# Gated DeltaNet branch: one set of scores for both directions, and the second triangular inverse on GpSimd

## The chip, the cores and the metric

One core of one Trainium2 chip runs the whole layer. The time is device time in microseconds (us), the median of three runs. 128 partitions; TensorE, VectorE (DVE), ScalarE (ACT), GpSimd (POOL) and SyncE (SP) each work through their own instructions in order and wait for each other by semaphores.

## The reference, cut to what matters

The reference is one layer of a bidirectional encoder: four branches over 1,024 tokens, a gated merge, cross-attention to a memory, a mixture of 32 experts. The change lies in branch D, the gated DeltaNet with four heads of 64, which runs over the sequence forward and backward and adds the two:

```python
kk = jnp.einsum('bhntd,bhnsd->bhnts', kc, kc)
a_mat = jnp.where(strict, bc[..., None] * kk * decay, 0.0) + jnp.eye(c)
sol = lax.linalg.triangular_solve(a_mat, rhs, left_side=True, lower=True, unit_diagonal=True)
qk = jnp.einsum('bhntd,bhnsd->bhnts', qc, kc) * decay
...
v_new = u_i - jnp.einsum('bhtd,bhde->bhte', kc_i, state)
o = jnp.einsum('bhtd,bhde->bhte', qd_i, state) + jnp.einsum('bhts,bhse->bhte', qk_i, v_new)
state = cd_i[..., None, None] * state + jnp.einsum('bhsd,bhse->bhde', kd_i, v_new)
```

For each chunk, the scores k k' and q k' are scaled by the decay exp(gam_t - gam_s) below the diagonal (above it, for the backward direction), a unit triangular matrix is inverted, and a recurrence carries the state from chunk to chunk. The scores of a chunk are the same for both directions; decay, mask and beta differ.

## The kernel before, in words

One list of steps, written by hand in `plan_schedule`, sets the order of every engine: each engine walks it and does its own part of each step. `dense(...)` interleaves the steps of a stage with the dense matmuls of other panels: each `None` in the list lets out one part, six matmuls of 128x512 for a `gate` (four parts a group) or `up` group (one part), with the ScalarE and VectorE work that belongs to it: weight conversion (L1349, L1965), the tanh of a gate (L1375), the eviction and addition of an `up` group (L1988, L1994). The two PSUM banks of the dense groups alternate, so TensorE waits when an eviction two groups back is late.

The DeltaNet works in eight chunks of 128 tokens, T/128 = `TT`. Three stages matter.

`gdn_a` prepares. In iteration i the forward direction has chunk i and the backward direction chunk 7 - i; each has PSUM banks of its own. GpSimd subtracts gamma from its broadcast row and masks the result (L2813, L2816, step part 0), ScalarE takes exp of it into `NQT` (L1716), TensorE makes the scores (L991, part 1), VectorE multiplies exp by beta (L2387) and both by the scores (L2395, marks `lt` and `qt`). `NLT` and `NQT` of one iteration lie in the buffer `LQ`, two of them in turn. ScalarE copies the 32x32 diagonal blocks out (L1728, part 2) and writes `LQ` to DRAM (`gdn_out`, L1763). Since exp writes into `NQT`, ScalarE waits in front of exp for the write of two iterations before (`lq_out`).

The inverse. The diagonal blocks of four iterations are a half b (0 or 1): `gdn_ship` writes them to DRAM (L1767), `gdn_read` reads them back with one block in each partition (L1777), `gdn_inv` inverts all 128 at once on VectorE, row by row:

```python
for j in range(first_row, next_row):
    n = 31 - j
    V.tensor_tensor(part, bc(U[:, j + 1:32, j:j + 1], P, n, j), bc(U[:, j:j + 1, 0:j], P, n, j), ALU.mult)
    V.tensor_tensor(U[:, j + 1:32, 0:j], U[:, j + 1:32, 0:j], part, ALU.subtract)
```

(L2407 and L2410, n times j elements a partition, 30 rows; each waits for the one before). Each half is cut into ten steps of three rows, in front a copy (L2402), at the end L2413, L2415 and two memsets. `gdn_back` writes the result to DRAM (L1783). Half 0 is inverted during `gdn_a` and after it, half 1 during the first three iterations of `gdn_c`.

`gdn_c` is the recurrence, eight iterations of seven parts. `gdn_load` and `gdn_load_inv` read `LQ` and the inverses from DRAM (L1793, and four issues of L1803 an iteration, all on ScalarE's queue). GpSimd spreads the 32x32 inverses into block diagonal matrices (L2825, part 0, two for each direction) and scales the keys (L2843, L2845, part 1); TensorE merges the blocks up to 128x128 (L1015, L1024, L1031, with a ScalarE copy L1751 in front of L1038) and does the products with the state (L1038 to L1066). Around the steps of `gdn_c` stands one None each, and in iterations 0 to 2 five more.

## Time and profile before

| what | us |
|---|---|
| median of three runs | 2041.04 (2040.80 to 2041.76) |
| the profiled execution, its own time | 2028.88 |
| its span | 2027.1 |
| TensorE busy | 1878.2 |
| VectorE, ScalarE, GpSimd busy | 1384.4, 1078.0, 308.8 |
| the stage `gdn_a`, first score matmul to last dense one before the next gap | 675.9 to 739.1 |
| the stage `gdn_c`, first matmul to last | 778.9 to 951.0 |

The profile records one execution. Busy time is what an engine spends in instructions; TensorE's ends are modelled. The mean granted clock of TensorE is 0.977 of full speed. Times in the rows below are counted from the start of the span. A wait is put down to what ended last before the engine went on.

### The profile page before, as it was taken

The page shows a single profiled execution, that of the slowest core. Times are in us where ns is not written, and L with a number is a line of the kernel's source. Part 1 is how long each engine was busy: PE and PEld are TensorE (multiplying, and loading weights), DVE is VectorE, ACT ScalarE, POOL GpSimd, SP SyncE. Part 2 cuts the span into 40 slices and gives each one's busy share as a digit, 9 for nine tenths or more (in the row PEclk, how much of TensorE's full clock was granted, in tenths as well). Part 3 has the DMA queues.
Part 4 walks back from the last instruction along what each step waited for, and adds up shares of the span by engine and source line. Part 5 has one row for each costly group of instructions (what it writes and reads, how often), then busy time and mean ns, then how long its engine had stood idle before and what let it go on. Part 6 is the DMA issues. An engine that isn't in the chain of part 4 may idle for free.

```text
span 2027.1 us, 32760 instructions
## 1 busy us (share of the span) xinstructions
PE 1878.2 (93%) x12949; PEld 1117.6 (55%) x12949; DVE 1384.4 (68%) x1833; ACT 1078.0 (53%) x1568; POOL 308.8 (15%) x269
## 2 busy tenths in 40 slices
PE   6999999999999989899999999995899999999991
PEld 3464565655544545677488755684455444444440
DVE  5555533799974797544733745437799999999997
ACT  4573223566646541223433533334588888888873
POOL 5000100344310512231000000000000111111103
PEclk9999999999999999999999999997899999999996
DMA  5411111212011562441522510404799999999986
GB/s 193 159 52 43 32 42 48 73 48 58 22 28 47 194 201 79 142 122 45 213 65 67 157 32 16 169 32 161 279 422 422 422 422 422 422 422 423 422 346 269
DMA packets 145817, 366.80 MB, mean 181 GB/s; under 512 B 39296, under 2 KB 94880, under 8 KB 119072
## 3 DMA queue, kind: packets, MB, share of 16 engines
q1 hardware_dynamic: 96608, 279.57, 36.3%
q10 hardware_dynamic: 40240, 52.50, 7.7%
q0 software_dynamic: 8848, 33.03, 4.2%
q8 instruction: 86, 1.41, 0.3%
q14 instruction: 35, 0.29, 0.0%
HBM read 314.14 MB, written 46.73 MB: 178 GB/s over the span
## 4 chain that ended last, share of the span: by engine, by line
PE 77%; DVE 10%; ACT 5%; issue 4%; DMA 2%; ACTq 1%; SPq 1%; DVEq 0%; POOLq 0%
PE psum L794 39%; PE psum L1185 24%; ACT arena L1631 2%; PE psum L1174 1%; PE psum L1109 1%; PE psum L1084 1%; DVE arena L2308 1%; PE psum L924 1%; PE psum L1203 1%; PE psum L811 1%; DMA gdn_lq<-arena 1%; PE psum L1066 1%; PE psum L1044 1%; DMA arena<-in_w_in_dram 1%; PE psum L935 1%
## 5 line engine op out<-in xcount | busy, mean ns | idle before, releaser
L794 PE MATMUL psum<-arena 128*128 128x512 f16 (+2 forms) x6000 | 1013.4, 326 | 17.6 <-ACT arena L1375 6.8
L794 PEld LDWEIGHTS psum<-arena 128*128 128x128 f16 x6000 | 567.6, 98 | 398.6 <-issue 15.6
L1185 PE MATMUL psum<-arena 128*128 128x512 f16 x2304 | 512.3, 381 | 14.7 <-issue 11.7
L751 DVE SCALAR_TENSOR_TENSOR arena<-arena 128x2048 f16<-128x2048 f32 x192 | 437.3, 2286 | 58.0 <-ACT arena L745 57.8
L745 ACT ACTIVATE arena<-arena 128x2048 f16<-128x2048 f32 x192 | 365.3, 1908 | 72.4 <-DMA arena<-in_w_dram 43.2
L1185 PEld LDWEIGHTS psum<-arena 128*128 128x128 f16 x2304 | 224.5, 98 | 280.4 <-issue 22.1
L1965 DVE SCALAR_TENSOR_TENSOR arena<-arena 128x512 f16<-128x512 f32 (+1 forms) x185 | 125.8, 699 | 114.0 <-ACT arena L1349 113.5
L2862 POOL DMA_INDIRECT arena<-xhat,arena x32 | 66.2, 2069 | 839.8 <-PE psum L1174 445.2
L1349 ACT ACTIVATE arena<-arena 128x512 f16<-128x512 f32 (+1 forms) x212 | 127.2, 616 | 51.5 <-issue 19.9
L1375 ACT ACTIVATE arena<-psum,arena 128x512 f32<-128x512 f32 x60 | 41.0, 684 | 140.3 <-PE psum L794 139.6
L1438 ACT ACTIVATE arena<-psum 128x512 f32<-128x512 f32 (+3 forms) x51 | 29.9, 586 | 126.4 <-PE psum L794 126.4
L1403 ACT ACTIVATE arena<-arena 128x256 f32<-128x256 f32 x64 | 26.7, 416 | 109.7 <-DVE arena L2000 108.6
L2757 POOL TENSOR_SCALAR arena<-arena 128x512 f32<-128x512 f32 x27 | 57.5, 2130 | 138.3 <-ACT arena L1349 138.3
L2293 DVE CUSTOM_DVE_ANT_0 arena<-psum,arena 128x1024 f32<-128x1024 f32 x64 | 75.6, 1219 | 2.3 <-PE psum L911 2.2
L1631 ACT ACTIVATE arena<-arena 128x1024 f32<-128x1024 f32 x64 | 72.9, 1147 | 7.3 <-DVE arena L2293 7.2
L1988 DVE SCALAR_TENSOR_TENSOR arena<-arena,psum 128x512 f32<-128x512 f32 x64 | 43.8, 684 | 42.7 <-PE psum L794 31.9
L2000 DVE SCALAR_TENSOR_TENSOR arena<-psum,arena 128x512 f32<-128x512 f32 x32 | 22.1, 690 | 65.1 <-PE psum L794 65.1
L2018 DVE SCALAR_TENSOR_TENSOR arena<-psum,arena 128x512 f16<-128x512 f32 x36 | 24.8, 690 | 59.9 <-ACT arena L1438 31.0
L1640 ACT ACTIVATE arena<-psum 128x512 f16<-128x512 f32 x64 | 34.7, 594 | 55.1 <-PE psum L924 34.3
L2825 POOL TENSOR_TENSOR arena<-arena 128x512 f32<-128x512 f32 x32 | 34.5, 1109 | 144.5 <-PE psum L1052 92.4
L1880 ACT ACTIVATE arena<-psum 128x512 f32<-128x512 f32 x64 | 38.2, 597 | 13.9 <-PE psum L1185 13.1
L1174 PE MATMUL psum<-arena 128*128 128x128 f32 x256 | 34.5, 279 | 8.8 <-DMA arena<-xhat,arena 8.8
(388 smaller groups left out, 2017.4 us busy)
## 6 DMA issues: line engine op xcount, KB each, us to landing
arena<-in_w_dram SPq DMA_DIRECT2D x192, 1024.0 KB, 11.9
arena<-in_merge_w_dram SPq DMA_DIRECT2D x64, 256.0 KB, 3.2
yrows<-arena ACTq DMA_DIRECT2D x32, 512.0 KB, 7.8
arena<-in_w_in_dram SPq DMA_DIRECT2D x48, 256.0 KB, 2.8
gdn_lq<-arena ACTq DMA_DIRECT2D x8, 1024.0 KB, 4.5
arena<-gdn_lq ACTq DMA_DIRECT2D x8, 1024.0 KB, 5.0
arena<-in_xattn_wkv_dram SPq DMA_DIRECT2D x32, 256.0 KB, 3.0
yrows<-arena POOLq DMA_DIRECT2D x1, 7680.0 KB, 24.1
```

The costliest lines, as they stand in the source:

```text
L745: nc.scalar.activation(half_of(pieces(e, m)[0], half), half_of(XLAND[m], half), ACT.Copy, scale=WS).then_inc(w_hi[m], 1)
L751: nc.vector.scalar_tensor_tensor(half_of(lo, half), half_of(XLAND[m], half), WS, half_of(hi, half), ALU.mult, ALU.subtract).then_inc(w_lo[ ...
L794: mm = nc.tensor.matmul(bank[prt[0]:prt[1], c0:c1], lhs[a](k), rhs[b](k), start=(k == 0 and a + b == 0), stop=(k == nk - 1 and a == 1))
L1174: tr = nc.tensor.transpose(PS[:, k // 4, (k % 4) * P:(k % 4) * P + P], xs[:, k, :], ident)
L1185: mm = nc.tensor.matmul(PS[:, bank, :], left[a][:, k, :], right[b][:, k, columns], start=k + a + b == 0, stop=(k == n - 1 and a == 1))
L1349: S.activation(W[i % 2][0][:, 2 * j:2 * j + 2, 0:wide], LAND[c % NLAND][:, :, 0:wide], ACT.Copy, scale=WS).then_inc(*act_hi.mark(c))
L1631: S.activation(DS[u % 2][:, m, :], DS[u % 2][:, m, :], ACT.Exp, scale=-1.0, bias=d_mx[u % 2][:, m:m + 1], accum_out=d_l[u % 2][:, m:m + 1])\
L1965: V.scalar_tensor_tensor(W[i % 2][1][:, 2 * j:2 * j + 2, 0:wide], LAND[c % NLAND][:, :, 0:wide], WS, W[i % 2][0][:, 2 * j:2 * j + 2, 0:wid ...
L1988: V.scalar_tensor_tensor(dst, gate, 1.0, bank, ALU.add, ALU.mult).then_inc(*e.mark(n))
L2293: V.tensor_tensor_reduce(out=DS[u % 2][:, m, :], in0=PS[:, 2 + 2 * m:4 + 2 * m, :].rearrange("p a b -> p (a b)"), in1=DWH[:, 896 - P * qt: ...
L2757: G.tensor_scalar(landed_c, landed_c, WS, None, ALU.mult).then_inc(*counter("pool_w_scaled").mark(chunk))
L2862: G.indirect_dma_start(XR[e % 2], None, XH_D, bass.IndirectOffsetOnAxis(IDX[:, e:e + 1], 0)).then_inc(rows_in[e % 2], 16)
```

## The change

- `gdn_a` takes one chunk an iteration for both directions, in the order `CH` = 0, 7, 1, 6, 2, 5, 3, 4. One set of scores is made for it; the banks now alternate by iteration. `AT` says in which iteration a chunk was prepared, and the writes of `LQ` and of the inverses and the rows of `GDIAG` are put so that `gdn_c` finds both directions of its iteration together. `gdn_out` issues two writes of half the size.
- exp goes into the buffer `NY`. ScalarE no longer waits there for `lq_out`, but for `qt` of the iteration before; VectorE waits for `lq_out` in front of its first product.
- `gdn_inv` of half 1 is one step of all thirty rows and runs on GpSimd. It stands behind `gdn_read` 1 and in front of `gdn_c` 0. `gdn_read` 1 moves up between the pieces of half 0; `gdn_back` 1 moves to iteration 0, part 3, and has four writes of 64 partitions, as has `gdn_back` 0.
- `gdn_load_inv` has two reads for each iteration instead of four.
- The Nones are dealt anew: more between the pieces of half 0, none extra in `gdn_c`.

The diff, with its indentation taken off and lines of context cut; the other hunks put the new marks and counts of the semaphores into waits:

```diff
@@ -260,19 +260,16 @@
...
 for i in range(TT):
-    mid = {6: inv(0, 2)}.get(i, [])
-    gdn += [("gdn_a", i, 1)] + {6: inv(0, 1), 7: inv(0, 4)}.get(i, []) + [None] + [("gdn_a", i + 1, 0), None] * (i + 1 < TT) + mid
-    gdn += [("gdn_a", i, 2), ("gdn_out", i)] + [("gdn_ship", 0)] * (i == 3) + [None]
-    gdn += {4: [("gdn_read", 0), None], 5: inv(0, 0) + [None], 6: inv(0, 3) + [None], 7: [("gdn_ship", 1)]}.get(i, [])
-for p in range(5, 10):
-    gdn += inv(0, p) + [None] * (2 + (p < 8)) + [("gdn_load", p - 5)] * (p < 7)
-gdn += [("gdn_back", 0)] + [None] * 6 + [("gdn_load_inv", 0), ("gdn_load_inv", 1), ("gdn_read", 1)] + [None] * 7
+    gdn += [("gdn_a", i, 1)] + {6: inv(0, 0), 7: inv(0, 2)}.get(i, []) + [None] + [("gdn_a", i + 1, 0), None] * (i + 1 < TT)
+    gdn += [("gdn_a", i, 2), ("gdn_out", i)] + {3: [("gdn_ship", 0)], 6: inv(0, 1), 7: [("gdn_ship", 1), None]}.get(i, []) + [None]
+    gdn += [("gdn_read", 0), None] * (i == 4) + [None] * (i >= 6)
+for p in range(3, 10):
+    gdn += inv(0, p) + [None] * (2 + (p > 3)) + [("gdn_load", p - 7)] * (p in (7, 8)) + [("gdn_read", 1), ("gdn_inv", 1, 1, 31)] * (p == 4)
+gdn += [("gdn_back", 0)] + [None] * 5 + [("gdn_load_inv", 0), ("gdn_load_inv", 1)] + [None] * 5
 for i in range(TT):
     for part in range(7):
-        gdn += [("gdn_back", 1)] * ((i, part) == (3, 1))
-        gdn += [("gdn_c", i, part)] + [None] * (1 + (i < 3 and part in (1, 4) and (i, part) != (2, 1)))
-        if i < 3 and part in (1, 2, 4) or (i, part) == (0, 5):
-            gdn += inv(1, 3 * i + (i > 0) + (1, 2, 4, 5).index(part))
+        gdn += [("gdn_back", 1)] * ((i, part) == (0, 3))
+        gdn += [("gdn_c", i, part), None]
         if part == 2 and i and i + 1 < TT:
@@ -467,6 +464,8 @@
...
 NGR = [[f32(BR + 8192 + 1024 * j + 512 * d, NH, P) for d in range(2)] if j < 2 else (NX, NZ_)[j % 2] for j in range(TT)]
+CH = [c for k in range(TT // 2) for c in (k, TT - 1 - k)]
+AT = [CH.index(i) for i in range(TT)]
 GDIAG = [f32(UN + 5120 + 1024 * b, 32, 32) for b in range(2)]
@@ -975,23 +974,21 @@
...
     q, v, a, po = (counter(f"{e}_gdn") for e in ("pe", "vec", "act", "pool"))
-    for d in range(2):
-        c = i if d == 0 else TT - 1 - i
-        cs = slice(c * P, c * P + P)
-        B0, B1, B2 = (PS[:, 2 + 3 * d + b, :].rearrange("p (h n) -> p h n", h=NH) for b in range(3))
-        if part == 1:
-            if i == 0 and d == 0:
-                pe.wait_ge(*counter("act_gdnp").at("tm", "nv", 3))
-                pe.wait_ge(*counter("act_gdnp").at("egrows"))
-            if i:
-                pe.wait_ge(*v.at("qt", i - 1, d))
-            for t in range(4):
-                for u, bank in enumerate((B1, B2)):
-                    hp = slice(64 * u, 64 * u + 64)
-                    mm = nc.tensor.matmul(bank[:, t, :], NK[hp, t % 2, cs], (NK if t < 2 else NQ)[hp, t % 2, cs],
-                                          start=True, stop=True)
-                    if t == 3:
-                        mm.then_inc(*q.mark("qk", i, d, u))
+    cs = slice(CH[i] * P, CH[i] * P + P)
+    B1, B2 = (PS[:, 3 + 3 * s + b, :].rearrange("p (h n) -> p h n", h=NH) for b in range(2))
+    if part == 1:
+        if i == 0:
+            pe.wait_ge(*counter("act_gdnp").at("tm", "nv", 3))
+            pe.wait_ge(*counter("act_gdnp").at("egrows"))
+        if i >= 2:
+            pe.wait_ge(*v.at("qt", i - 2, 1))
+        for t in range(4):
+            for u, bank in enumerate((B1, B2)):
+                hp = slice(64 * u, 64 * u + 64)
+                mm = nc.tensor.matmul(bank[:, t, :], NK[hp, t % 2, cs], (NK if t < 2 else NQ)[hp, t % 2, cs],
+                                      start=True, stop=True)
+                if t == 3:
+                    mm.then_inc(*q.mark("qk", i, u))
 elif what == "gdn_c":
@@ -1434,7 +1431,7 @@
...
             elif name == "nz":
-                act.wait_ge(inv_out[1], 32)
+                act.wait_ge(inv_out[1], 64)
         S.activation(dst, src, ACT.Copy, scale=1 / WS).then_inc(*e.mark(n))
@@ -1703,29 +1700,32 @@
...
         for d in range(2):
-            r0 = 32 * d + 4 * (j if d == 0 else TT - 1 - j)
+            r0 = 32 * d + 4 * CH[j]
             S.dma_start(NGR[j][d], A["gdn_rows"][0, r0:r0 + 4].partition_broadcast(P)).then_inc(gam_in[j], 16)
...
         for d in range(2):
-            c = i if d == 0 else TT - 1 - i
             act.wait_ge(*po.at("low", i, d))
-            after(act, lq_out[i % 2], 16 * (i // 2))
-            S.activation(NQT[i % 2][d], NGR[i][d], ACT.Exp).then_inc(*a.mark("dt", i, d))
+            if i:
+                act.wait_ge(*v.at("qt", i - 1, d))
+            else:
+                act.wait_ge(*counter("act_gdnp").at("tm", "nv", 3))
+            S.activation(NY[d], NGR[i][d], ACT.Exp).then_inc(*a.mark("dt", i, d))
         j = i + 2
...
                 act.wait_ge(*(a.at("dt", j - 2, d) if j >= 4 else counter("act_gdnp").at("tm", "nv", 3)))
-                r0 = 32 * d + 4 * (j if d == 0 else TT - 1 - j)
+                r0 = 32 * d + 4 * CH[j]
                 S.dma_start(NGR[j][d], A["gdn_rows"][0, r0:r0 + 4].partition_broadcast(P)).then_inc(gam_in[j % 2], 16)
...
                 bp = slice(32 * b, 32 * b + 32)
-                S.activation(GDIAG[i // 4][bp, 16 * d + 4 * (i % 4):16 * d + 4 * (i % 4) + 4, :], NLT[i % 2][d][bp, :, bp], ACT.Copy)\
+                u0 = 16 * d + 4 * ((i ^ d) % 4)
+                S.activation(GDIAG[i // 4][bp, u0:u0 + 4, :], NLT[i % 2][d][bp, :, bp], ACT.Copy)\
                     .then_inc(*a.mark("diag", i, d, b))
@@ -1760,7 +1760,8 @@
...
     act.wait_ge(*counter("vec_gdn").at("qt", i, 1))
-    S.dma_start(A["gdn_lq"][i], LQ[i % 2]).then_inc(lq_out[i % 2], 16)
+    for d in range(2):
+        S.dma_start(A["gdn_lq"][i ^ d, :, 1024 * d:1024 * d + 1024], LQ[i % 2][:, 1024 * d:1024 * d + 1024]).then_inc(lq_out[i % 2], 16)
 elif what == "gdn_ship":
@@ -1778,30 +1779,31 @@
...
     b = step[1]
-    act.wait_ge(*counter("vec_gdn").at("inv", b))
+    act.wait_ge(*counter("pool_gdn" if b else "vec_gdn").at("inv", b))
     for n, m in enumerate((NU[b], NUT[b])):
-        S.dma_start(A["gdn_inv"][b, n].rearrange("u (b f) -> (u b) f", b=4), m.rearrange("p r c -> p (r c)")).then_inc(inv_out[b], 16)
+        for d in range(2):
+            S.dma_start(A["gdn_inv"][b, n].rearrange("(k e h) (b f) -> e k (h b) f", e=2, h=NH, b=4)[d],
+                        m[64 * d:64 * d + 64].rearrange("p r c -> p (r c)")).then_inc(inv_out[b], 16)
 elif what == "gdn_load":
...
     q = counter("pe_gdn")
-    act.wait_ge(lq_out[s], 16 * TT // 2)
+    act.wait_ge(lq_out[s], 32 * TT // 2)
     if i < 2:
...
         act.wait_ge(*q.at("o", i - 2, 1))
-    S.dma_start(LQ[s], A["gdn_lq"][i]).then_inc(lq_in[s], 16)
+    S.dma_start(LQ[s], A["gdn_lq"][AT[i]]).then_inc(lq_in[s], 16)
 elif what == "gdn_load_inv":
...
     s = i % 2
-    act.wait_ge(inv_out[i // 4], 32)
+    b, k = divmod(AT[i], 4)
+    act.wait_ge(inv_out[b], 64)
     if i >= 2:
...
     for n in range(2):
-        for d in range(2):
-            u0 = 16 * d + 4 * (i % 4)
-            S.dma_start(XZC[s][:, 8 * n + 4 * d:8 * n + 4 * d + 4, :],
-                        A["gdn_inv"][i // 4, n, u0:u0 + 4].rearrange("u (p c) -> p u c", c=32)).then_inc(lq_in[s], 16)
+        S.dma_start(XZC[s][:, 8 * n:8 * n + 8, :],
+                    A["gdn_inv"][b, n, 8 * k:8 * k + 8].rearrange("u (p c) -> p u c", c=32)).then_inc(lq_in[s], 16)
 elif what == "merged_pair":
@@ -2378,22 +2380,21 @@
...
     for d in range(2):
-        c = i if d == 0 else TT - 1 - i
-        B1, B2 = (PS[:, 3 + 3 * d + b, :].rearrange("p (h n) -> p h n", h=NH) for b in range(2))
         if part == 1:
...
                 dve.wait_ge(*a.at("diag", i - 2, d, 3))
-            V.tensor_tensor(NLT[s][d], NQT[s][d], bc(BES[:, d, c, :].unsqueeze(2), P, NH, P), ALU.mult)\
+                dve.wait_ge(lq_out[s], 32 * (i // 2))
+            V.tensor_tensor(NLT[s][d], NY[d], bc(BES[:, d, CH[i], :].unsqueeze(2), P, NH, P), ALU.mult)\
                 .then_inc(*v.mark("dt1", i, d))
             dve.wait_ge(*v.last())
-            BB = PS[:, 3 + 3 * d:5 + 3 * d, :]
+            BB = PS[:, 3 + 3 * s:5 + 3 * s, :]
             for u in range(2):
-                dve.wait_ge(*q.at("qk", i, d, u))
-            for n, (of, to) in enumerate((("lt", NLT), ("qt", NQT))):
-                both = to[s][d].rearrange("p (u t) n -> p u (t n)", u=2)
-                V.tensor_tensor(both, BB[:, :, 256 * n:256 * n + 256], both, ALU.mult).then_inc(*v.mark(of, i, d))
-elif what == "gdn_inv":
+                dve.wait_ge(*q.at("qk", i, u))
+            for n, (of, to, by) in enumerate((("lt", NLT[s][d], NLT[s][d]), ("qt", NQT[s][d], NY[d]))):
+                to, by = (m.rearrange("p (u t) n -> p u (t n)", u=2) for m in (to, by))
+                V.tensor_tensor(to, BB[:, :, 256 * n:256 * n + 256], by, ALU.mult).then_inc(*v.mark(of, i, d))
+elif what == "gdn_inv" and not step[1]:
     b, first_row, next_row = step[1:]
@@ -2815,6 +2816,30 @@
...
                             pattern=[[0, NH], [-1 if d else 1, P]], channel_multiplier=1 if d else -1).then_inc(*po.mark("low", i, d))
+elif what == "gdn_inv" and step[1]:
+    b, first_row, next_row = step[1:]
+    po = counter("pool_gdn")
+    U, UT = NU[b], NUT[b]
+    if first_row == 1:
+        pool.wait_ge(diag_in[b], 32)
+        pool.wait_ge(*counter("act_gdn").at("dt", TT - 1, 1))
+        G.tensor_copy(U[0:64], UT[0:64].rearrange("p r c -> p c r")).then_inc(*po.mark("forward", b))
+        pool.wait_ge(*po.last())
+    for j in range(first_row, next_row):
+        n = 31 - j
+        part = NX[0].rearrange("p h n -> p (h n)")[:, 0:n * j].rearrange("p (r c) -> p r c", c=j)
+        G.tensor_tensor(part, bc(U[:, j + 1:32, j:j + 1], P, n, j), bc(U[:, j:j + 1, 0:j], P, n, j), ALU.mult)\
+            .then_inc(*po.mark("term", b, j))
+        pool.wait_ge(*po.last())
+        G.tensor_tensor(U[:, j + 1:32, 0:j], U[:, j + 1:32, 0:j], part, ALU.subtract).then_inc(*po.mark("row", b, j))
+        pool.wait_ge(*po.last())
+    if next_row == 31:
+        G.tensor_scalar(UT, U.rearrange("p r c -> p c r"), -1.0, None, ALU.mult).then_inc(*po.mark("turned", b))
+        pool.wait_ge(*po.last())
+        G.tensor_scalar(U, U, -1.0, None, ALU.mult).then_inc(*po.mark("negative", b))
+        pool.wait_ge(*po.last())
+        for m in (U, UT):
+            G.memset(m.rearrange("p r c -> p (r c)")[:, ::33], 1.0).then_inc(*po.mark(*(("inv", b) if m is UT else ("one", b))))
 elif what == "gdn_c":
```

## Rows read from the trace of the kernel before

**Rows 1.** The page: TensorE's busy share, and the chain by engine.

```profile
PE 1878.2 (93%) x12949; PEld 1117.6 (55%) x12949; DVE 1384.4 (68%) x1833; ACT 1078.0 (53%) x1568; POOL 308.8 (15%) x269
...
PE 77%; DVE 10%; ACT 5%; issue 4%; DMA 2%; ACTq 1%; SPq 1%; DVEq 0%; POOLq 0%
```

**Rows 2.** Windows: us, busy us (instructions) per engine, granted clock, DMA share, GB/s.

```profile
675.90:739.10 63.20, 57.00 (x431) 32.94 (x430) 52.68 (x84) 31.37 (x80) 24.32 (x25) 0.97 0.61 200
739.10:745.30 6.20, 0.06 (x2) 0.03 (x2) 5.92 (x13) 4.18 (x11) 0.00 (x0) 0.94 0.40 148
...
778.90:802.90 24.00, 24.00 (x275) 15.93 (x275) 19.76 (x51) 4.93 (x11) 6.47 (x8) 1.00 0.14 46
...
912.10:932.20 20.10, 20.10 (x273) 17.81 (x273) 8.59 (x25) 5.26 (x12) 6.42 (x9) 1.00 0.35 107
932.20:951.00 18.80, 18.80 (x259) 16.84 (x259) 7.36 (x21) 3.38 (x8) 1.13 (x2) 1.00 0.03 9
```

**Rows 3.** TensorE's waits from 675 to 955: us in total, times, longest.

```profile
PE psum L794 <- DVE arena L1988: 6.1, 1, 6.1
PE psum L1038 <- ACT arena L1751: 5.2, 3, 2.2
PE psum L794 <- ACT arena L1375: 4.9, 2, 2.6
PE psum L991 <- DVE arena L2395: 3.6, 4, 1.3
```

**Rows 4.** Timeline of TensorE: start, us, instructions, [idle before <- releaser].

```profile
722.78 2.06 PE L991 MATMUL psum<-arena 64*128 64x128 f32 x32
...
745.28 28.67 PE L794 MATMUL psum<-arena 128*128 128x512 f16 x126 [6.14 <-DVE arena L1988]
```

**Rows 5.** All waits from 675 to 955, ScalarE's for the write.

```profile
ACT arena L1716 <- DMA gdn_lq<-arena: 15.0, 6, 3.7
```

**Rows 6.** Timeline of VectorE in gdn_a.

```profile
677.86 1.11 DVE L2387 TENSOR_TENSOR arena<-arena 128x512 f32<-128x512 f32 x1
...
682.44 0.95 DVE L2387 TENSOR_TENSOR arena<-arena 128x512 f32<-128x512 f32 x1
...
687.44 0.69 DVE L1994 TENSOR_TENSOR arena<-arena 128x512 f32<-128x512 f32 x1
...
716.99 1.34 DVE L1994 TENSOR_TENSOR arena<-arena 128x512 f32<-128x512 f32 x1
...
740.70 1.29 DVE L2395 TENSOR_TENSOR arena<-psum,arena 128x512 f32<-128x512 f32 x2
```

**Rows 7.** DMA issues from 660 to 960: count, KB each, median us to landing.

```profile
gdn_lq<-arena ACTq DMA_DIRECT2D x8, 1024.0 KB, 4.5
...
gdn_diag<-arena ACTq DMA_DIRECT2D x2, 512.0 KB, 6.6
arena<-gdn_diag ACTq DMA_DIRECT2D x4, 256.0 KB, 5.0
```

**Rows 8.** Timeline of GpSimd in two stretches.

```profile
16.20 1.48 POOL L2757 TENSOR_SCALAR arena<-arena 128x512 f32<-128x512 f32 x1
17.77 1.91 POOL L2759 TENSOR_TENSOR arena<-arena 128x512 f16<-128x512 f32 x1
...
716.75 1.04 POOL L2813 TENSOR_TENSOR arena<-arena 128x512 f32<-128x512 f32 x1 [5.35 <-DMA arena<-gdn_rows]
...
847.89 0.61 POOL L2843 TENSOR_TENSOR arena<-arena 128x256 f32<-128x256 f32 x1 [0.67 <-DVE arena L2451]
...
864.80 4.03 POOL L2825 TENSOR_TENSOR arena<-arena 128x512 f32<-128x512 f32 x4 [13.96 <-PE psum L1052]
```

**Rows 9.** Groups on VectorE from 720 to 765: busy, mean ns, idle before.

```profile
L2410 DVE TENSOR_TENSOR arena<-arena 128x30 f32<-128x30 f32 (+14 forms) x30 | 10.0, 332 | 1.0
L2407 DVE TENSOR_TENSOR arena<-arena 128x30 f32<-128x30 f32 (+14 forms) x30 | 9.9, 330 | 0.8
```

**Rows 10.** Window just behind the gap that ends at 745.3.

```profile
745.00:746.00 1.00, 0.72 (x2) 0.28 (x3) 0.96 (x3) 0.00 (x0) 0.00 (x0) 0.50 0.95 275
```

8 lines of the change are left out of this document (4 added, 4 removed).

## The prediction

> **What bounds the kernel now.** I read the page's busy shares and its chain first: TensorE is busy 93% of the span and carries 77% of the chain [rows 1]. So a change pays only where it removes work from TensorE or closes a gap in it. Then the table of windows over the DeltaNet stage [rows 2]. Its preparation (`gdn_a`, 675.9 to 739.1) has 57.00 us of TensorE in 63.20, and the next window is a pure gap of 6.2. The recurrence (`gdn_c`, 778.9 to 951.0, eight windows) costs 24.0 us in its first iteration, 20.1 when undisturbed and 18.8 in the last. The list of TensorE's waits [rows 3] says which waits end last: 6.1 us on VectorE's eviction of an `up` group, queued behind pieces of the first inverse; 4.9 and 3.6 on ScalarE and VectorE while `gdn_a` runs; 5.2 on the ScalarE copy L1751, behind which stand the issues of reads. Together about 21 us of idle time. ScalarE itself waits six times for the write of `gdn_lq` [rows 5].
>
> **Fill.** Each None of the order lets out six matmuls (128x512), 1.28 us when they stream: 126 of them took 28.67 us [rows 4], of which about 1.5 us was the low level of the clock. I counted the Nones from `gdn_a` 0 to the last `gdn_c`: 117 in both orders. So the fill is moved, not added, and the time changes by TensorE's saved work plus the difference in its gaps.
>
> **1. One set of scores.** An iteration issues 16 instead of 32 score matmuls. 32 took 2.06 us [rows 4], so half is 0.95 to 1.03 and eight iterations save about 8 us of TensorE.
>
> **2. Exp into NY, no wait for the DMA in front of it.** Before, ScalarE issued the write of `gdn_lq`, waited for its landing and only then did exp, the diagonal copies and the next write: `gdn_a` ran at about 8.5 us an iteration (`qt` 0 ends at 682.4, `qt` 7 at 742.0, [rows 6]). After it, exp waits for VectorE's `qt` of the iteration before, and VectorE waits for the write of two iterations before. VectorE's own work is then 4.6 us (from one L2387 to that of the next iteration, [rows 6], iteration 0) plus 1.2 for evictions and low parts of three Nones, 5.8 in all. The DMA loop needs 0.65 exp, some 1.0 until the write is issued, 4.5 to land [rows 7] and 4.6 of VectorE over two iterations, so it hardly binds; at worst (6.5 an iteration) it costs 5 us more. The doubled write issues are ScalarE sequencer time beside its own diagonal copies: nothing, at most a microsecond in all. From 682.4, six iterations on is 717.2; then two pieces of inverse 0 (copy 1.1 and twelve short operations, 4.9) and the last iteration: `qt` 7 at 727.5 instead of 742.0. TensorE gains some of this at once, but what counts is what is late next.
>
> **3. The second inverse on GpSimd.** It stands in GpSimd's queue in front of the spreads L2825 of `gdn_c` 0, and TensorE waits for those. So its length decides. Its start: diagonal copies about 1 us after `qt` 7, the ship to DRAM 6.6, the read back issued and landed, 5.0 plus 1 for its second half [rows 7]: 727.5 + 14 to 15 = about 742.
> Its length: for j = 1 to 30 two operations of j(31-j) elements each, 60 instructions and 9,920 elements. The trace has no such short GpSimd operation. The nearest rows are tensor_tensors of 256 elements at 0.61 us and of 512 at 1.04 [rows 8], so 1.68 ns an element and 0.18 fixed; a dependent one starts 0.08 later (16.20 + 1.48 to 17.77). 60 x 0.26 + 16.7 = 32.3 us. The pattern broken in runs of 32 (L2825, four in 4.03) is no slower; runs of one to 30 are not shown. The two closing tensor_scalars of 1,024 elements follow L2757, 1.48 for 512: 2.8 each. Copy and memsets 1.8. Sum 40 us alone. From below I take 36 (closing ones and gaps cheap), from above 62 (short runs at a little over half the rate).
> Contention: L1994 on VectorE took 1.34 us instead of 0.69 (as at 687.44) because it stood until GpSimd's L2813 had ended [rows 6, 8]; so the two exclude each other for operations with two SBUF inputs. During GpSimd's first 24 us VectorE still does 30 operations of inverse 0 (60 of them are 19.9 us, [rows 9]). If they take turns, each GpSimd operation loses about 0.2: 6 us. Later evictions cost 2 more. I take 48.5, and add 2 for the first two spreads: `gdn_c` 0 starts on TensorE at 742 + 48.5 + 2 = 793.
> The Trainium skill (SBUF — State Buffer, the part on the shared port pair) says the pair is an exclusive lock held for a whole instruction; the trace agrees in L1994's 1.34 us, and it speaks against moving an inverse beside the other.
>
> **4. What covers it.** From `gdn_read` 1 to `gdn_c` 0 lie 25 Nones, 32 us. TensorE reaches the read at about 735 and `gdn_c` 0 at 768. Inverse 0, slowed by the turns, ends at about 763; its write and reads, at 4 to 5 us each like those of [rows 7], and their issue allow the start at 775 at the latest, so it stays in front of GpSimd. TensorE stands 20 to 25 us. After such a gap the granted clock is low (0.50 behind the gap of 6.1 us, [rows 10]) and gives away 1.5 us more.
>
> **5. The recurrence.** VectorE loses 20 us of inverse work there, but was not its bound: the fill removed (five Nones, 6.4 us) is time that TensorE spent earlier. Of the 6.2 us of gaps, fewer reads (two instead of four issues an iteration) and a free VectorE take 4; the four issues of `gdn_back` 1, now in front of L1751 in iteration 0, give 1.5 back. 172.1 - 6.4 - 2.5 = 163.2.
>
> **Sum.** 793 + 163.2 + 1.5 = 957.7 where the recurrence ended at 951.0: +6.7 us. Behind it everything shifts along. On the profiled span 2027.1 becomes 2033.8 (its time 2028.88 becomes 2035.6). The profiled execution lies 12 us under the median of the runs; I put the difference on the median: 2041 + 7 = 2048.
>
> **Rivals.**
> A, my forecast: GpSimd's inverse is later than its cover. 2048, own range 2042 to 2056. Chance 0.48.
> B, the other side: the inverse on GpSimd is done in 30 us or less, or nearly so. Then inverse 0's way through DRAM sets the start at about 773 and the end is 773 + 163.2 = 936 to 938: -13, 2028. It decides below 42 us of length, where the sum is nil. For it speaks that the row of 0.61 us may hold more pipeline time than I think, and that some closing operations are single-input; against, that 16.7 us for the elements alone is measured rate. Chance 0.28 for the side below 42, some of it near no change.
> C, short runs cost extra on GpSimd: 62 us, `gdn_c` 0 at 806, +20, 2061. Nothing in the trace shows runs under 32. Chance 0.16.
> The Trainium skill (GPSIMD Engine Reference, section 3.1) states 2.6 cycles an element at 1.2 GHz for two inputs, 2.17 ns; the trace shows 1.68 ns. As an estimate by that page the elements take 21.5 us instead of 16.7 and the end is 2053, between A and C.
> D, `gdn_a` is not quicker, because ScalarE, now held by VectorE's `qt`, or the write still sets 8 us an iteration: everything in A starts 10 us later, 2058. For it speaks that out, exp and `dt1` still form a loop over two iterations; against, the sum of 13 us or less for two. Chance 0.08.
>
> **Numbers.** 0.2% is 4 us, about what a measurement of this kernel can tell from no change. A lies above it in about 0.38 and within it in 0.10; B faster in 0.23, within in 0.05; C and D slower. Faster 0.24, same 0.16, slower 0.60. The range takes both ends of the length, from B's 2029 to C's 2062.
>
> **What would show it.** Right: L991 with 128 instructions; no wait of L1716 for `gdn_lq`; `qt` 7 near 728; the GpSimd chain from about 742 for 45 to 55 us without a gap; one TensorE wait of 20 us or more on GpSimd in front of the first L1015; recurrence of 162 to 164 us. Wrong: GpSimd operations of 240 elements far from 0.58 us, no such wait, or `gdn_a` still at 8 us an iteration.

## The result, and the profile after

The changed kernel takes 2072.72 us (median of 4 runs, 2071.38 to 2075.02) against 2040.92 for the kernel before (4 runs, 2037.04 to 2041.76). The ratio is 1.0153, with a 95% interval of 1.0127 to 1.0178: 26 to 36 us slower. The prediction was 2048, with a range of 2029 to 2062: the sign was right, the size was not, and the time lies above the range. The profiled execution has a span of 2070.4 us (its time 2072.16).

Where the time lies is read off the stage's ends. In the windows below gdn_c ends at 977.0, where it was 951.0: +26.0 of the stage. What comes behind can't be compared between these two profiled executions: from there to the end of the span it is 1076.1 us before and 1093.4 after, but among the experiments below, which change next to nothing there, it lies between 1078 and 1093 (1089.6 in before_two_exp, the kernel nearest to before). So 26 us are located and the rest of the median's 31.8 (some 5 us, no more than the interval leaves open) is not.

The windows of the stage (us; busy us and instructions of TensorE, its weight loads, VectorE, ScalarE, GpSimd; granted clock as a share of full speed; DMA share; GB/s): gdn_a, the way to gdn_c 0, gdn_c 0, gdn_c 1, and the other six.

```profile
678.00:744.20 66.20, 48.29 (x264) 22.33 (x263) 45.94 (x76) 32.84 (x85) 23.67 (x24) 0.85 0.64 191
744.20:807.90 63.70, 46.47 (x189) 19.05 (x188) 43.29 (x75) 10.54 (x19) 45.21 (x68) 0.89 0.47 128
807.90:836.10 28.20, 23.48 (x227) 15.24 (x227) 8.55 (x23) 3.73 (x9) 10.26 (x13) 0.88 0.14 48
836.10:857.00 20.90, 20.45 (x229) 14.13 (x229) 9.05 (x24) 5.57 (x12) 6.43 (x9) 1.00 0.41 114
857.00:977.00 120.00, 119.09 (x1442) 91.33 (x1442) 48.72 (x136) 28.06 (x61) 34.50 (x42) 1.00 0.35 104
```

Against [rows 2] TensorE has less to do in gdn_a, as meant, but the stretch is no shorter and its clock is 0.85 instead of 0.97. It then takes 63.7 us from the last `qt` to gdn_c 0, where it took 37 (742.0 to 778.9). gdn_c 0 costs 28.2 instead of 24.0.

TensorE's waits from 675 to 1010 (us in total, times, longest), and three waits of the others from 675 to 808:

```profile
PE psum L793 <- ACT arena L1372: 26.4, 6, 6.2
PE psum L793 <- DVE arena L1990: 8.1, 2, 5.4
PE psum L1035 <- ACT arena L1751: 4.0, 2, 3.1
PE psum L1012 <- POOL arena L2850: 2.0, 2, 1.6
```

```profile
DVE arena L1967 <- ACT arena L1346: 38.5, 8, 10.9
...
ACT arena L1715 <- DVE arena L2396: 26.2, 11, 4.6
...
ACT arena L1372 <- issue: 15.8, 2, 14.4
```

[Rows 3] held four small waits; now one line dominates, ScalarE's gate tanh L1372: 17.9 of its 26.4 us lie in gdn_a (four times), 8.5 on the way to gdn_c 0 (twice). GpSimd, which was to be the late one, has 2.0 us. ScalarE waits for VectorE's `qt` in front of exp (L1715), VectorE waits for ScalarE's high part L1346 (18.6 of the 38.5 us up to the last `qt`), and nobody waits for the write of `gdn_lq` any more, as ScalarE did in [rows 5]. "issue" means that the profile shows no wait; the 14.4 us in front of L1372 are explained further down.

One iteration of gdn_a, all engines (start, us, what; idle before and releaser in brackets):

```profile
695.50 1.29 DVE L2396 TENSOR_TENSOR arena<-psum,arena 128x512 f32<-128x512 f32 x2
...
696.88 0.63 ACT L1715 ACTIVATE arena<-arena 128x512 f32<-128x512 f32 x1 [2.10 <-DVE arena L2396]
696.90 0.96 ACTq L1721 DMA_DIRECT2D arena<-gdn_rows  x2
...
697.91 1.30 ACT L1728 ACTIVATE arena<-arena 32x128 f32<-32x128 f32 x4 [0.40 <-ACT arena L1715]
...
699.57 0.97 ACT L1728 ACTIVATE arena<-arena 32x128 f32<-32x128 f32 x3
700.57 0.63 ACT L1346 ACTIVATE arena<-arena 128x512 f16<-128x512 f32 x1
701.10 0.67 ACT L1372 ACTIVATE arena<-psum,arena 128x512 f32<-128x512 f32 x1
701.23 0.69 DVE L1967 SCALAR_TENSOR_TENSOR arena<-arena 128x512 f16<-128x512 f32 x1 [4.44 <-ACT arena L1346]
...
701.83 1.03 PE L793 MATMUL psum<-arena 128*128 128x512 f16 x2 [6.10 <-ACT arena L1372]
701.84 0.68 DVE L2388 TENSOR_TENSOR arena<-arena 128x512 f32<-128x512 f32 x1
```

This is a ring. (A None's weight conversion has a high part on ScalarE, L1346, and a low part on VectorE, L1967, which waits for it. Line numbers shift by a few from kernel to kernel.) The last `qt` (to 696.8) lets exp go; behind exp in ScalarE's order stand the issues, the eight diagonal copies and the high part; VectorE, whose low part L1967 stands ahead of its next `dt1`, has nothing to do for 4.44 us; TensorE, whose next group needs the gate tanh, nothing for 6.10. Then VectorE works and ScalarE waits. `dt1` starts at 682.2, 692.1, 701.8 and 711.6: 9.8 us an iteration. That is the ring's own pace. Not every iteration has it: the second `qt` comes only 4.0 us behind the first, and the fifth iteration takes 12.3 us, with slower issues of `gdn_rows` (1.90 us) and the two of `gdn_read` (2.2) in ScalarE's order. From the first iteration's `qt` to the last, seven iterations take 8.8 us each on average, where they took 8.5 before.

The second inverse on GpSimd (first instructions, the middle, the end), and ScalarE's queue around the two writes of inverses:

```profile
757.75 1.94 POOL L2826 COPY arena<-arena 64x1024 f32<-64x1024 f32 x1 [31.09 <-DMA arena<-gdn_diag]
759.78 0.29 POOL L2831 TENSOR_TENSOR arena<-arena 128x30 f32<-128x30 f32 x1
...
777.54 0.61 POOL L2831 TENSOR_TENSOR arena<-arena 128x240 f32<-128x240 f32 x1
778.23 0.65 POOL L2834 TENSOR_TENSOR arena<-arena 128x240 f32<-128x240 f32 x1
...
780.48 1.29 POOL L2831 TENSOR_TENSOR arena<-arena 128x238 f32<-128x238 f32 x1
...
798.79 3.63 POOL L2837 TENSOR_SCALAR arena<-arena 128x1024 f32<-128x1024 f32 x1
802.50 3.04 POOL L2839 TENSOR_SCALAR arena<-arena 128x1024 f32<-128x1024 f32 x1
```

```profile
782.59 5.08 ACTq L1785 DMA_DIRECT2D gdn_inv<-arena  x4
799.12 2.39 ACTq L1805 DMA_DIRECT2D arena<-gdn_inv  x4
...
817.86 4.91 ACTq L1785 DMA_DIRECT2D gdn_inv<-arena  x4
```

GpSimd needs 757.75 to 805.8, 48.0 us, with the durations that the prediction gave it. But the second fence holds what it did not see: four writes, each of 64 partitions of one of the two matrices, keep ScalarE's issue for 5.08 us, and from the first of them to the first read that waits for them are 16.5 us. The kernel before issued two writes (0.82 us at 763.93) and the reads 4.7 us later. ScalarE stands in this stretch twice: before 782.6 it waits some 9 us for VectorE's first inverse, which with the 5.08 us of issues makes the 14.4 us "issue" in front of L1372; and from 789.0 to 799.1 it waits for the writes to land, and can do no high part meanwhile.

### The profile page after: what moved, and what is told of

Same layout as the page of the kernel before. It is cut to its first block, busy times and chain, and to the rows that moved or that the text cites. A ratio compares the mean times of both kernels' runs of the same rounds, so it can differ in the third digit from the quotient of the medians.

```text
span 2070.4 us, 32498 instructions
## 1 busy us (share of the span) xinstructions
PE 1884.4 (91%) x12821; PEld 1112.7 (54%) x12821; DVE 1365.5 (66%) x1768; ACT 1079.2 (52%) x1568; POOL 348.8 (17%) x334
## 4 chain that ended last, share of the span: by engine, by line
PE 76%; DVE 8%; ACT 5%; issue 5%; POOL 2%; DMA 2%; ACTq 1%; DVEq 1%; SPq 1%; POOLq 0%
PE psum L793 38%; PE psum L1182 24%; ACT arena L1628 2%; PE psum L1171 1%; PE psum L1106 1%; PE psum L1081 1%; DVE arena L2310 1%; POOL arena L2831 1%; PE psum L923 1%; POOL arena L2834 1%; ACT arena L1728 1%; PE psum L1200 1%; PE psum L810 1%; PE psum L1063 1%; PE psum L1041 1%
## 5 line engine op out<-in xcount | busy, mean ns | idle before, releaser
L793 PE MATMUL psum<-arena 128*128 128x512 f16 (+2 forms) x6000 | 1029.0, 329 | 41.2 <-ACT arena L1372 28.3
L750 DVE SCALAR_TENSOR_TENSOR arena<-arena 128x2048 f16<-128x2048 f32 x192 | 437.3, 2286 | 57.6 <-ACT arena L744 57.5
L1967 DVE SCALAR_TENSOR_TENSOR arena<-arena 128x512 f16<-128x512 f32 (+1 forms) x185 | 123.2, 686 | 138.0 <-ACT arena L1346 137.6
L2887 POOL DMA_INDIRECT arena<-xhat,arena x32 | 65.5, 2048 | 842.2 <-PE psum L1171 445.9
L1346 ACT ACTIVATE arena<-arena 128x512 f16<-128x512 f32 (+1 forms) x212 | 127.0, 616 | 60.6 <-issue 24.7
L1372 ACT ACTIVATE arena<-psum,arena 128x512 f32<-128x512 f32 x60 | 41.0, 684 | 152.6 <-PE psum L793 136.7
L1990 DVE SCALAR_TENSOR_TENSOR arena<-arena,psum 128x512 f32<-128x512 f32 x64 | 43.8, 684 | 40.2 <-PE psum L793 26.9
```

Of the source, the lines that this page charges most:

```text
L750: nc.vector.scalar_tensor_tensor(half_of(lo, half), half_of(XLAND[m], half), WS, half_of(hi, half), ALU.mult, ALU.subtract).then_inc(w_lo[ ...
L793: mm = nc.tensor.matmul(bank[prt[0]:prt[1], c0:c1], lhs[a](k), rhs[b](k), start=(k == 0 and a + b == 0), stop=(k == nk - 1 and a == 1))
L1346: S.activation(W[i % 2][0][:, 2 * j:2 * j + 2, 0:wide], LAND[c % NLAND][:, :, 0:wide], ACT.Copy, scale=WS).then_inc(*act_hi.mark(c))
L1967: V.scalar_tensor_tensor(W[i % 2][1][:, 2 * j:2 * j + 2, 0:wide], LAND[c % NLAND][:, :, 0:wide], WS, W[i % 2][0][:, 2 * j:2 * j + 2, 0:wid ...
L1990: V.scalar_tensor_tensor(dst, gate, 1.0, bank, ALU.add, ALU.mult).then_inc(*e.mark(n))
L2887: G.indirect_dma_start(XR[e % 2], None, XH_D, bass.IndirectOffsetOnAxis(IDX[:, e:e + 1], 0)).then_inc(rows_in[e % 2], 16)
```

## The experiments

Each was timed in at least three rounds against the kernel before on the same chip; chips differ by up to 9 us (before: 2031 to 2040), so ratios are compared; the times in the expectations are meant for a kernel before of about 2040. A ratio's interval is about 0.0016 to either side (the widest are the changed kernel's own, 0.0026, and flat_back's, 0.0024). So a difference from the changed kernel is known to about 0.003: two_exp, undo_exp and vec_inverse are just clear of it, flat_back and short_pool are not, and rest on their traces, of one execution each. "From dt1" is a time counted from the first `dt1` of that run's trace, which lies between 677 and 683. One thousandth is 2 us.

| kernel | ratio | last `qt` | gdn_c 0 | gdn_c's end |
|---|---|---|---|---|
| before | 1 | 64.1 | 101 | 273.1 |
| changed | 1.0153 | 66.2 | 129.9 | 299.0 |
| two_exp | 1.0116 | 56.7 | 120.1 | 289.0 |
| undo_exp | 1.0118 | 62.5 | 125.9 | 294.8 |
| vec_inverse | 1.0116 | 66.3 | 119.1 | 297.6 |
| flat_back | 1.0126 | 64.9 | 128.8 | 295.0 |
| short_pool | 1.0137 | 66.6 | 130.1 | 295.8 |
| short_pool_flat | 1.0073 | 65.0 | 118.1 | 280.5 |
| both | 1.0064 | 55.9 | 109.0 | 286.1 |
| both_flat | 1.0062 | 57.8 | 102.2 | 287.0 |
| pool_flat_two | 1.0104 | 56.4 | 120.0 | 287.5 |
| spread | 1.0023 | 57.8 | 99.0 | 280.0 |
| spread2 | 1.0020 | 58.7 | 100.7 | 281.5 |
| scores_only | 1.0060 | 63.5 | 105.2 | 285.6 |
| after_twice | 1.0149 | 66.3 | 129.8 | 298.6 |
| spread_twice | 1.0036 | 57.5 | 98.9 | 281.2 |
| before_two_exp | 1.0000 | 62.2 | 99.4 | 273.2 |

(the last three columns are us from dt1)

**two_exp.** A second pair of exp buffers.

```
+ NE_ = (NY, [f32(BR + 10752 + 512 * d, NH, P) for d in range(2)])
- if i: act.wait_ge(*v.at("qt", i - 1, d))
- S.activation(NY[d], NGR[i][d], ACT.Exp)
+ if i >= 2: act.wait_ge(*v.at("qt", i - 2, d))
+ S.activation(NE_[i % 2][d], NGR[i][d], ACT.Exp)
```

> The changed kernel with exp written alternately into NY and into a second pair of buffers (the space of XZC, not in use yet), so that exp of iteration i waits for qt of i-2 instead of i-1; nothing else differs. Theory 1 (the single NY ties ScalarE and VectorE into one chain: qt, exp, diagonal copies, eviction, dt1): an iteration of gdn_a falls from 9.8 us to 6 to 7.5, qt 7 ends near 730 instead of 744, GpSimd's inverse starts near 743 instead of 757.8, and the first gdn_c matmul comes 12 to 14 us earlier; time 2058 to 2062. Theory 2 (the write of gdn_lq sets the iteration, through VectorE's wait for it): no change of the iteration, 9.8 us, and the time stays within 3 us of 2072. Theory 3 (the start of gdn_c does not follow qt 7 at all, since inverse 0 and its way through DRAM set it): the iteration falls but the time stays near 2070.

Measured: 2061.97, ratio 1.0116. The last `qt` comes 9.5 us earlier (at 735.1, not near 730) and gdn_c 0 9.8 us earlier, less than the 12 to 14 expected. `dt1` starts at 682.2, 690.7, 697.0 and 704.6, which is 6.4 to 8.5 us an iteration; over all seven the mean is 7.5. Theory 1 holds for the most part: the write of `gdn_lq` is as it was, and VectorE's wait for it did not hold the iteration. The 5.8 us of the prediction is not reached here either; the fifth iteration takes 11.6 us, and in it two issues hold ScalarE's queue for 5.7 us, of which more under the hardware.

**undo_exp.** The other direction: exp back into `NQT`, behind the write.

```
- act.wait_ge(*v.at("qt", i - 1, d))
- S.activation(NY[d], NGR[i][d], ACT.Exp)
+ after(act, lq_out[i % 2], 32 * (i // 2))
+ S.activation(NQT[i % 2][d], NGR[i][d], ACT.Exp)
```

> The changed kernel with exp as before: written into the iteration's own NQT buffer, ScalarE waiting for the write of gdn_lq two iterations before, and VectorE not waiting for it. Shared scores, the inverse on GpSimd and the new layout stay. Theory 1 (the single NY is what holds gdn_a at 9.8 us an iteration): the iteration is 8 to 8.8 us again, as before the change, qt 7 ends near 734 to 738 instead of 744.2, and the time is 2062 to 2067. Theory 2 (the iteration is long for another reason, such as the two half writes or the shared banks): it stays at 9.8 us and the time at 2072.

Measured: ratio 1.0118 (interval 1.0101 to 1.0136) against the changed kernel's 1.0153. The last `qt` comes 3.7 us earlier, gdn_c 0 4.0; `dt1` starts at 681.6, 691.3, 700.4 and 709.1, 9.1 us an iteration and a little over the range expected, as is the last `qt` (739.8). The mean over all seven is 8.3. So the exp edit, as it was made, cost some 7 us by the ratios and 4 by the traces: the wait that it brought is worse than the one that it took away.

**vec_inverse.** The second inverse on VectorE, its ten pieces ahead of gdn_c 0.

```
- + [("gdn_read", 1), ("gdn_inv", 1, 1, 31)] * (p == 4)
- gdn += [("gdn_back", 0)] + [None] * 5 + [loads of 0 and 1] + [None] * 5
+ + [("gdn_read", 1)] * (p == 4)
+ gdn += [("gdn_back", 0)]
+ for p in range(10):
+     gdn += inv(1, p) + [None] + [loads of 0 and 1] * (p == 4)
```

> The changed kernel with the second inverse on VectorE, in ten pieces right behind the first, one with each of the ten sixfold groups of matmuls ahead of gdn_c 0; exp and the scores stay as changed. If GpSimd's inverse sets the start of gdn_c 0 (807.9 in the changed kernel) and slows the first one by turns: the first inverse ends near 770 instead of 782.4, the second takes about 22 us and ends near 795, gdn_c 0 starts at 795 to 799 and the time is 2060 to 2065; some of that is given back if VectorE's pieces delay evictions (TensorE waits on L1990). If the inverse on GpSimd is harmless (the gap comes from gdn_a alone): no change or slower, since VectorE now has 22 us more in front of gdn_c.

Measured: 2063.99, ratio 1.0116. The first inverse, with no inverse on GpSimd beside it, ends 94.9 from dt1 instead of 104.4, and gdn_c 0 starts at 119.1 instead of 129.9. But gdn_c then has 178.5 us instead of 169.1: TensorE waits 9.5 us once, for VectorE's evictions in gdn_c 0 (L2431), which stand behind the second inverse, and that ends at 809.8, not at 795. So the start was won and most of it given back, and the trace's end is only 1.4 us earlier; the ratio says 7.6.

**both.** The two edits together.

> Both edits: second exp buffer and the second inverse on VectorE behind the first. If the two losses are one behind the other, the gains add: gdn_c 0 starts near 783 and ends near 948, time 2045 to 2050. If they overlap (whichever is late alone sets the start), the time is that of the better of the two, 2058 to 2062.

Measured: 2053.5, ratio 1.0064; gdn_c 0 at 787.8 (109.0), end at 964.9. The gains add within the intervals (0.0037 and 0.0037 make 0.0074, measured 0.0089), but the time is 3 us above the range expected and the end 17 us behind the expected 948. The same wait is there again (9.3 us). TensorE's waits in both, from 675.9 on:

```profile
PE psum L796 <- ACT arena L1375: 15.4, 5, 5.5
PE psum L1024 <- DVE arena L2432: 9.3, 1, 9.3
PE psum L1038 <- ACT arena L1754: 4.1, 2, 3.2
```

**short_pool.** Rows 16 to 30 of the second inverse left out on GpSimd: `for j in range(first_row, 16)`.

> The changed kernel with rows 16 to 30 of the second inverse left out on GpSimd (30 of 60 short operations; half 1's inverse is then incomplete). By the trace they take 16 us. If GpSimd's length sets the start of gdn_c 0, it comes 10 to 16 us earlier (the way of inverse 0 through DRAM can bind at about 797) and the time is 2057 to 2063. If it does not, the time stays at 2072.

Measured: 2067.25, ratio 1.0137. GpSimd is done at 786.1, some 20 us earlier, and gdn_c 0 is not a microsecond earlier (130.1 from dt1). The end is 3.2 us earlier all the same: gdn_c is shorter (165.7 us), and no run says why. These rows of GpSimd say what holds gdn_c 0:

```profile
785.85 0.21 POOL L2842 MEMSET arena<- 128x32 f32 x2
802.79 3.94 POOL L2850 TENSOR_TENSOR arena<-arena 128x512 f32<-128x512 f32 x3 [16.73 <-DMA arena<-gdn_inv]
```

The spread now waits 16.73 us for the first inverse's way through DRAM. So my theory that GpSimd alone sets the start fell: beside it, only 3 us earlier (802.8 against 805.7), stood a second chain: the read of inverse 0 is issued at 799.6 here and at 799.1 in the changed kernel.

**flat_back.** The inverses written and read as before the change.

```
- for d in range(2):
-     S.dma_start(A["gdn_inv"][b, n].rearrange("(k e h) (b f) -> e k (h b) f", e=2, h=NH, b=4)[d], m[64 * d:64 * d + 64]...)
+ S.dma_start(A["gdn_inv"][b, n].rearrange("u (b f) -> (u b) f", b=4), m.rearrange("p r c -> p (r c)"))
```

> The changed kernel with the two inverses written to DRAM as before: one write of 128 partitions for each matrix instead of two of 64 in a three-level pattern, and read back by four issues instead of two. Theory 4: the new pattern keeps most DMA engines idle, so that inverse 0 needs 16.5 us from the first write's issue to the first read's instead of 4.7, and ScalarE is blocked meanwhile. Then this interval is 5 to 6 us here, the four issues of back 1 no longer stand 4.9 us in front of L1751, and TensorE's waits on ScalarE shrink by 3 to 8 us; gdn_c 0 itself starts at 804 to 807, since GpSimd's inverse still ends near 805; time 2064 to 2069. If the pattern costs nothing, the interval stays at 16 us and the time at 2072, or rises by the added read issues.

Measured: ratio 1.0126. From the first write's issue (780.06) to the first read's (784.10) are 4.0 us instead of 16.5. This answers to it: the window of that interval in the changed kernel, then in flat_back (clock, DMA share and GB/s are the last three).

```profile
782.50:799.10 16.60, 11.08 (x36) 4.03 (x36) 4.81 (x7) 1.20 (x2) 14.47 (x28) 0.79 0.30 95
```

```profile
780.00:784.10 4.10, 3.43 (x11) 1.36 (x12) 4.07 (x6) 1.21 (x2) 3.73 (x5) 0.73 0.71 274
```

The same megabyte leaves with the DMA engines busy for 0.71 of their time in one pattern, and for 0.30 in the other. The queue of these writes, in the changed kernel (782 to 799) and in flat_back (780 to 784.1), as packets, MB and share of the 16 DMA engines' time:

```profile
q10 hardware_dynamic: 272, 1.05, 18.2%
```

```profile
q10 hardware_dynamic: 288, 1.05, 64.7%
```

Both are 256 packets of 4 KB, each of 159 ns (median). The rest are packets of 4 bytes: 16 for the four new writes, 32 for the two old ones, so four and sixteen a write. Of this queue mostly three to four packets are in flight at a time in the changed kernel and never more than six, in flat_back mostly sixteen. So theory 4 holds: the packets are no slower, but the new writes, all four together, run some four side by side, where the old ones run sixteen. Now GpSimd alone is late in front of gdn_c 0, and the gap that the prediction expected there is seen, with 12.9 us:

```profile
PE psum L793 <- ACT arena L1372: 17.0, 4, 7.0
PE psum L1012 <- POOL arena L2850: 14.2, 2, 12.9
```

gdn_c 0 starts only 1.1 us earlier, as expected. The other 2.9 of the 4.0 us that the trace shows (5.5 by the ratios) are gained in gdn_c, where two issues (0.8 us) instead of four stand in front of L1751 and TensorE's wait for it falls from 3.1 to 2.3. That this is all of it is not shown: short_pool has a gdn_c as short with all four issues.

**short_pool_flat.** Both last edits.

> The changed kernel with two edits together: rows 16 to 30 of the second inverse left out on GpSimd (as in short_pool), and the inverses written and read as before the change (as in flat_back). Alone the first gave a ratio of 1.0137 and the second 1.0126, the changed kernel 1.0153. Theory: two chains end within some 3 us of each other in front of gdn_c 0, GpSimd's inverse and inverse 0's way through DRAM, so each repair alone shows the other. Then both together bring the first gdn_c matmul from 128 to 130 us behind the first dt1 to 110 to 117, and the ratio to 1.004 to 1.008. If the gains only add (0.0016 and 0.0027), the ratio is 1.011.

Measured: ratio 1.0073 (1.0057 to 1.0090). Singly they gave 0.0016 and 0.0027, together 0.0080, some 16 us: two chains side by side, either of which hides what shortening the other gains. The ratios alone would barely tell this from a plain sum; the traces do: gdn_c 0 is at 118.1 (just above the range expected), 11.8 us earlier, where the single edits gave -0.2 and 1.1. What GpSimd's spread waits for now is the first inverse's way through DRAM, 5.5 us.

**both_flat** and **spread.** Second exp buffer, second inverse on VectorE, flat writes; in spread the pieces of the second inverse stand apart:

```
+ gdn += inv(1, p // 3) * (p % 3 == 0 and p < 9) + [None] + ...
+ gdn += [("gdn_c", i, part), None] + {(0, 1): inv(1, 3), (0, 2): inv(1, 4), ..., (0, 6): inv(1, 8), (1, 0): inv(1, 9)}.get((i, part), [])
```

> Second exp buffer, second inverse on VectorE behind the first, and the inverses written and read as before. Against the kernel with the first two edits alone (2053.5): theory 4 gives gdn_c 0 at 780 to 783 instead of 787.8 and no 3.2 us wait behind back 1's issues, but the wait of 9.3 us on VectorE's second inverse grows; 2045 to 2050. If only the order of VectorE's work sets the end there, it stays at 2053.

> As the kernel before it in this list, with the second inverse's ten pieces spread: three among the ten groups of matmuls ahead of gdn_c 0, seven among parts of gdn_c 0 and the first of gdn_c 1; its write to DRAM ahead of part 2 of gdn_c 1. If the rest of the loss is the second inverse standing in front of VectorE's evictions for gdn_c, the wait of 9.3 us goes, gdn_c takes 165 to 168 us from about 780, and the time is 2036 to 2043, about that of the kernel before. If the pieces only move the wait, 2045 to 2050.

Measured: both_flat 1.0062, against 1.0064 for both. gdn_c 0 starts at 102.2 instead of 109.0, and the one wait on VectorE grows from 9.3 to 17.2 us and eats all of it: my expected 2045 to 2050 was wrong, though I had named the wait. spread: 1.0023 (1.0008 to 1.0037), some 2045.6 on the scale of 2041: the better of my two outcomes (2036 to 2043, gdn_c 165 to 168 us) did not come, the other one did. gdn_c 0 at 99.0, earlier than before's 101, gdn_c 181 us. These are the longest of TensorE's waits in spread:

```profile
PE psum L797 <- ACT arena L1376: 8.3, 3, 5.4
PE psum L1059 <- DVE arena L2446: 4.9, 1, 4.9
PE psum L1016 <- DVE arena L2440: 3.8, 1, 3.8
```

The second and the third stand behind pieces of the second inverse in VectorE's order.

**spread2.** Five pieces ahead of gdn_c 0, five in it, four more groups of matmuls beside those.

> The kernel spread with five instead of three pieces of the second inverse ahead of gdn_c 0, five in gdn_c 0 and the start of gdn_c 1, and four more groups of six matmuls beside those (they are then missing from later stages, none is added). In spread TensorE still waits 4.9 us on vn and 3.8 on the z of gdn_c 1, each behind pieces of the inverse. If these waits go, the ratio is 0.998 to 1.001. If VectorE is simply full there (its 23 us of inverse in 41 us), it stays at 1.002.

Measured in five rounds: 1.0020 (1.0010 to 1.0031). The waits move (6.8 us on L2433 in gdn_c 0, 1.8 on L2440) and the sum stays. This is the best of the versions with shared scores that were tried, and none of them beats the kernel before.

**pool_flat_two.** All mended but the second inverse, which stays on GpSimd.

> The changed kernel with the second exp buffer and the old layout of the written inverses; the second inverse stays on GpSimd. Against spread (1.0023) it tells what the inverse on GpSimd costs when all else is mended. GpSimd's inverse starts 14 us behind the last qt and takes 46 to 48 us: the first gdn_c matmul at 118 to 121 us behind the first dt1 (99 in spread), with a TensorE wait of 12 to 20 us on the spread in front of it; gdn_c then takes 166 us instead of 181. Ratio 1.006 to 1.009.

Measured: ratio 1.0104, above the range expected, gdn_c 0 at 120.0 as expected. TensorE waits once for 11.5 us on the spread L2851 (12.8 in all), and gdn_c takes 167.5. Against spread, whose pieces are also dealt better, the inverse on GpSimd costs 0.0081, some 16 us. That is the largest of the differences measured for one part of the change. In the changed kernel, vec_inverse gave only 0.0037 for it, with its pieces in one block.

**scores_only.** spread, with exp as before the change. Of the change it keeps the shared scores and their order of chunks, and with them the two half writes of `gdn_lq`; the Nones and the pieces of both inverses are still dealt as in spread, not as before.

> The kernel spread (ratio 1.0023) with exp as before the change too: into NQT, behind the write of gdn_lq. Of the change it keeps only the shared scores and the chunk order that they bring. If ScalarE's wait for the write costs gdn_a its pace, the iteration is 8 to 8.5 us against 7.2 to 8 with two buffers, and the ratio is 1.003 to 1.006. If the exp edit is worth nothing with two buffers either, the ratio is 1.002. If the shared scores had brought their 8 us of TensorE, it would be under 1.000.

Measured: ratio 1.0060 (1.0043 to 1.0077). Exp in two buffers is worth 0.0037 in this order. A kernel that has of the change's ideas only the shared scores is not faster, but slower; how much of that is the chunk order, the half writes or the dealing of the pieces is not separated. An iteration takes 9.2 us (`dt1` from the second iteration to the last), above the 8 to 8.5 that I expected.

**after_twice** and **spread_twice.** Every score matmul issued twice.

```
- for t in range(4):
+ for t8 in range(8):
+     t = t8 % 4
```

> The changed kernel with every score matmul issued twice into the same place (32 instead of 16 an iteration, as many as before the change), nothing else. If the saved TensorE work is worth its 8 us, the ratio rises from 1.0153 to 1.019. If gdn_a's pace is set by VectorE and ScalarE, TensorE only stands still in the time saved: the ratio stays at 1.014 to 1.016, and TensorE's busy time between the first dt1 and the last qt rises by 6 to 8 us while its idle time falls as much.

> The kernel spread (1.0023) with every score matmul issued twice. There gdn_a runs at VectorE's pace with two exp buffers and TensorE is busy 49 of 57 us. If the saved scores are worth their 8 us there, the ratio is 1.006; if half of it, 1.004; if nothing, 1.002 to 1.003.

Measured: after_twice 1.0149 (1.0133 to 1.0165), the changed kernel 1.0153; spread_twice 1.0036 (1.0015 to 1.0058), spread 1.0023. The windows from the first `dt1` to the last `qt` of after_twice, for which the changed kernel's is the first of the windows above:

```profile
681.90:747.60 65.70, 54.72 (x395) 30.18 (x392) 45.73 (x75) 33.04 (x84) 24.12 (x24) 0.90 0.62 193
```

This window stops short of the last `qt`, which ends at 748.3; up to there TensorE is busy 55.4 us of 66.4. So it is 7.1 us busier than in the changed kernel, and the stretch has the same length. The trace shows nothing that the saved matmuls were worth in the changed kernel, and the ratios leave at most some 5 us; in spread it is 0.0013, which is within the intervals.

**before_two_exp.** The kernel before, with exp in two buffers and the wait for the write on VectorE, as in two_exp.

> The kernel before with one edit: exp goes alternately into NY and a second pair of buffers, ScalarE waits for qt two iterations before and VectorE, not ScalarE, for the write of gdn_lq. Scores, chunk order, schedule and inverses stay as before. ScalarE's six waits of 15.0 us in all go. If they set gdn_a's pace there, qt 7 comes 3 to 6 us earlier, and the first inverse with it; but gdn_c 0 starts with TensorE's fill (it hardly waits there in the kernel before), so the gain is what goes of the 14 us of TensorE waits in gdn_a: 2 to 5 us, ratio 0.9975 to 0.999. If TensorE's own work sets it, 1.000.

Measured in five rounds: 1.0000 (0.9988 to 1.0013). The six waits of [rows 5] are gone, and the stage's first seven iterations take 58.3 us instead of 60.2 from the first `dt1` to the last iteration's; but gdn_c 0 starts at 99.4 against 101 and its end (273.2) is where it was. These waits cost nothing there that can be measured (the interval is 2.5 us to either side). My 2 to 5 us were wrong.

## Why the prediction was wrong

**Fill, and step 1 (scores, 8 us).** The count of matmuls is right (half as many). What was wrong is the sentence that the time changes by TensorE's saved work plus its gaps, with the gaps then estimated on their own. In gdn_a the ring through ScalarE and VectorE sets the pace, so every matmul taken from TensorE becomes a gap (after_twice), and the granted clock is lower with more gaps: 0.97 before, 0.85 in the changed kernel, 0.90 with the scores twice. The 16 matmuls of an iteration take 1.16 us, not 0.95 to 1.03; eight iterations save some 7 us of TensorE's work.

**Step 2 (an iteration of 5.8 us, the last `qt` at 727.5) is the step that failed.** Measured 9.8 us in the ring, 8.8 as the mean of seven, and 744.2. I added VectorE's own work (4.6 + 1.2) and asked only whether the DMA loop was longer. I wrote myself that exp waits for VectorE's `qt` of the iteration before, but did not follow the loop that this closes: `qt`, exp, and then, in ScalarE's order, issues, diagonal copies and the high part, for which VectorE waits ahead of its next `dt1`. Its sum stands in the timeline above, 696.8 to 701.8, 5.0 us, beside VectorE's 4.8. My "at worst 6.5" came from the wrong loop. undo_exp and two_exp show it from both sides: either the wait for the write or a second buffer is better than this one. But the ring is not all of the 16.7 us by which the last `qt` is late: the second buffer takes 9.5 of them away and leaves a mean of 7.5 us. Part of the rest stands in the fifth iteration, with the issues behind the ship and the two reads of `gdn_diag` in ScalarE's order; the prediction's sum has no term for them, and no run takes them out.

**Step 3 (GpSimd's start and length).** The start was put 14.5 us behind the last `qt`, and it is 13.5; the length 48.5, and it is 48.0; the spreads 2.0 and 2.1. 744.2 + 13.5 + 48.0 + 2.1 = 807.9. gdn_c 0 is 14.9 us later than my 793: 16.7 from step 2, and the other terms, with the rounding, give 1.8 back. Inside, the terms shift a little: operations of 240 elements take 0.61 and 0.65 where my line gave 0.58, those of 30 0.24 to 0.37; the closing two took 3.6 and 3.0 instead of 2.8 each; contention is seen singly on GpSimd's side (1.29 instead of 0.61). It is VectorE that loses throughout: beside GpSimd's chain its operations of 30 to 150 elements take 0.63 to 0.72 us (all but the last), where operations of the same sizes took 0.20 to 0.32 ahead of it, and without GpSimd's chain (vec_inverse) the first inverse ends 9.5 us earlier. From 30 to 240 elements the rows rise by 1.8 to 1.9 ns an element (0.24 to 0.61, 0.25 to 0.65). The Trainium skill (GPSIMD Engine Reference, section 3.1) has 2.6 cycles, which at its 1.2 GHz is 2.17 ns; the rows lie between it and the 1.68 that I took.

**Step 4 (inverse 0's way allows the start at 775; the gap is 20 to 25 us).** Wrong in its first half: the first inverse ended at 782.4 instead of 763, again step 2 for the most part, and its way through DRAM took some 20 us instead of 12, since I priced the new writes like the old: 16.5 until the reads are issued at 799.1, and the last of them landed some 3 us later, if they took what they took in short_pool. That is 3 us ahead of GpSimd. So the price was hidden behind GpSimd at the start of gdn_c 0, and short_pool fell into just this. It was not hidden elsewhere: ScalarE, issuing the writes and waiting for their landing, left its part of the dense groups undone, and TensorE stood 8.5 us for L1372 there, beside 8.1 us for VectorE's evictions L1990 behind the first inverse's pieces. So the gap before gdn_c 0 came scattered, and not as one wait for GpSimd (2.0). flat_back brings the predicted wait back, with 12.9 us. Clock: I took 1.5 us; the granted clock was 0.85 to 0.89 for 130 us. What that cost is not isolated: in gdn_a, where TensorE stands anyway, 0.90 in after_twice made nothing shorter.

**Step 5 (163.2 + 1.5).** Measured 169.1. The four issues of back 1 take 4.9 us in front of L1751 (TensorE waits 3.1), and gdn_c 0 runs at a clock of 0.88: 28.2 us, where before it took 24.0 with more fill. The other seven take 140.9. The four issues cost more than the 1.5 us that I gave them, and the second spread is 1.6 late; what is left of the 4.4 us over the forecast is not attributed.

**The sum.** gdn_c ends at 977.0 instead of 957.7: 14.9 by its start and 4.4 by its length. The median is 24.7 us above the forecast; the other 5 lie behind the stage and are not located. (The chances of the prediction add up to 0.62 for slower and 0.23 for faster, by its own parts, not 0.60 and 0.24.) The likeliest case, A, had the right sign but not the main mechanism. Rival D (chance 0.08) was it: gdn_a is no quicker, with ScalarE held by VectorE's `qt`. Its 2058 is still 15 us short: the last `qt` is 16.7 us later than in A and not the 10 that D adds, gdn_c is 4.4 longer, and some 5 us are not located. That D stood in the list at 0.08 is no credit to the forecast, since its sum was made without the ring. Rivals B and C are refuted by GpSimd's 48.0 us.

**What it comes to.** Repairs from the changed kernel's 1.0153: a second exp buffer 0.0037; the flat writes 0.0027; both, and the second inverse back on VectorE and spread, 0.0130 together. Of the remaining 0.002 I can only argue the cause: with shared scores the chunks come in pairs from both ends, so the recurrence needs the second half's inverse at its third iteration, not at its fifth, and VectorE must be done with its 20 us within two iterations, where before it had nearly three. The waits behind its pieces (8.7 us in spread) fit that, and moving the pieces (spread2) moved the waits only. It was not isolated, nor were the half writes of `gdn_lq`: a kernel that shares the scores in the old order of halves was not tried.

## What to carry to other kernels

When an edit swaps one wait for another, write down the loop that the new wait closes, with everything that the in-order engines have queued inside it; the sum of that loop, not the busiest engine's work, is the new iteration. Work removed from the busiest engine is worth nothing in a stretch whose pace such a loop sets. Where two parallel chains end close together, shortening one moves next to nothing: take both away once before saying which one is the bound. And price a changed access pattern as a new DMA, even if its bytes are the same.

## What the runs showed of the hardware

- Writing 64 partitions to DRAM in a pattern of three levels (4 x 16 x 1,024 elements), four times 256 KB, took 16.5 us from first issue to the end of waiting, at a DMA share of 0.30; two writes of 128 partitions, the same megabyte, took 4.0 us at 0.71. The 4 KB packets take 159 ns in both; in the first pattern mostly three to four are in flight, of all four writes together, in the second mostly sixteen. The slowest level of the first pattern has four steps, which fits the four, but no run varies it. Each of the four issues also held ScalarE 1.2 to 1.3 us, instead of 0.4.
- A DMA issue can hold its engine for microseconds. In two_exp two issues of `gdn_rows` right behind the ship of `gdn_diag` (702.18, 512 KB) kept ScalarE's queue for 5.67 us, where they take 0.8 otherwise. All eight traces in which they start 1.9 to 2.3 us behind the ship show 3.5 to 7.5 us; where they start 4.0 to 6.4 us behind it (before, changed, undo_exp, scores_only), they take 1.0 to 1.9. No run takes the ship away, so that it is the cause is argued:

```profile
702.18 1.08 ACTq L1769 DMA_DIRECT2D gdn_diag<-arena  x1
704.48 5.67 ACTq L1722 DMA_DIRECT2D arena<-gdn_rows  x2
```

- TensorE's granted clock was lower where it stood more: from the first `dt1` to gdn_c's end it is busy 257.79 us in the changed kernel at a mean granted clock of 0.93, and 252.26 before at 0.99, although the changed kernel has 128 matmuls fewer. Whether such a loss lengthens a stretch depends on what sets its pace; in gdn_a it did not (after_twice).
- One VectorE operation of 234 elements beside GpSimd's copy took 2.14 us (L2408 at 757.82), the next of that size 0.40: it stood until GpSimd's 1.94 us were over, although that copy has one input and 64 partitions only. Beside GpSimd's chain of short two-input operations, VectorE's last ones, of 150 down to 30 elements, took 0.63 to 0.72 us each, which is about the length of the GpSimd operations (0.61 to 0.75) that ran then, and a last one of 30 took 0.19.
